# Context product of the projection blocks: one matmul of 128 weight columns, or two of 64 columns

## The reference, cut to what matters

```python
h = rms_norm(x, norm1_g) * (1 + sc1) + sh1
z = h @ w_in
conv_a, conv_g, q, k, v = jnp.split(
    z, [D_CONV, 2 * D_CONV, 2 * D_CONV + D_QK, 2 * D_CONV + 2 * D_QK], axis=-1)
```

## Time and profile before

| | |
|---|---|
| median of 3 runs | 1809.16 us (1808.12 to 1811.60) |
| profiled execution, first to last instruction (span) | 1807.7 us |
| TensorE busy | 1619.1 us, 90% |
| VectorE / ScalarE / GpSimd busy | 829.0 / 572.2 / 391.3 us |
| projection blocks (L649, L705) | 1024 passes |

### The profile page before, as it was taken

The page is one execution under the profiler, slowest core; times in us unless marked ns, Lnnn a source line. Parts: engine busy times, 40 slices in busy tenths (PEclk is TensorE's granted clock), DMA queues, the critical chain, the costliest instruction groups (busy, mean ns, idle before and its releaser), DMA issues. The chain is left out here.

```text
span 1807.7 us, 69734 instructions
## 1 busy us (share of the span) xinstructions
PE 1619.1 (90%) x27905; PEld 1281.1 (71%) x27905; DVE 829.0 (46%) x2593; ACT 572.2 (32%) x2228; POOL 391.3 (22%) x2166
## 2 busy tenths in 40 slices
PE   6999988986999999888869999899599998998885
PEld 3554457446999989888735554664389988998885
DVE  2299768262333323232245996943623232423233
ACT  2200245235545432211130003542355554221211
POOL 1100000002343424332310000000124333333332
PEclk9999999997999999999989999999799999999998
DMA  9356640237999999999953412221599999999992
GB/s 348 129 184 235 233 174 1 105 127 284 402 409 409 409 409 409 409 409 409 361 206 140 157 58 102 108 94 35 202 374 409 409 409 409 408 409 409 409 407 111
DMA packets 146722, 502.59 MB, mean 278 GB/s; under 512 B 6217, under 2 KB 6642, under 8 KB 146578
## 3 DMA queue, kind: packets, MB, share of 16 engines
q1 hardware_dynamic: 142288, 488.96, 69.5%
q0 software_dynamic: 3264, 10.88, 1.8%
q10 hardware_dynamic: 1026, 1.25, 0.2%
HBM read 494.76 MB, written 6.31 MB: 277 GB/s over the span
## 5 line engine op out<-in xcount | busy, mean ns | idle before, releaser
L950 PE MATMUL ps<-v_sb,weight_ring 128*64 128x80 f32 x16384 | 589.3, 234 | 51.7 <-DMA weight_ring<-in_w_gate_dram 20.8
L950 PEld LDWEIGHTS ps<-v_sb,weight_ring 128*64 128x64 f32 x16384 | 577.3, 138 | 63.0 <-DMA weight_ring<-in_w_gate_dram 25.0
L967 PE MATMUL ps<-v_sb,weight_ring 128*64 128x80 f32 x8192 | 296.7, 234 | 31.7 <-DVE v_sb L1693 19.9
L967 PEld LDWEIGHTS ps<-v_sb,weight_ring 128*64 128x64 f32 x8192 | 288.4, 138 | 40.0 <-DVE v_sb L1693 25.0
L705 PE MATMUL ps<-mix,weight_ring 128*128 128x128 f32 (+1 forms) x976 | 271.0, 439 | 2.1 <-ACT mix L1054 1.2
L1238 ACT ACTIVATE v_sb<-mix 128x8 f32 x1520 | 185.5, 205 | 223.6 <-PE ps L950 146.1
L1719 DVE TENSOR_TENSOR qk<-qk,v_sb 128x8 f32 x1520 | 212.3, 194 | 90.8 <-issue 90.0
L1848 POOL COPY v_sb<-mix 128x8 f32 x1040 | 145.2, 198 | 479.0 <-PE ps L950 417.7
L1861 POOL TENSOR_TENSOR qk<-qk,v_sb 128x8 f32 x1040 | 198.7, 232 | 181.7 <-DVE v_sb L1708 178.5
L705 PEld LDWEIGHTS ps<-mix,weight_ring 128*128 128x128 f32 x976 | 148.1, 194 | 122.8 <-issue 119.8
L1443 DVE SCALAR_TENSOR_TENSOR weight_ring<-u_gate,conv_cols,weight_ring 128x655 f32<-128x655 f32 x240 | 195.3, 899 | 0.0
(11 more groups left out here) (195 smaller groups left out, 1240.5 us busy)
## 6 DMA issues: line engine op xcount, KB each, us to landing
weight_ring<-in_w_down_dram SPq DMA_DIRECT2D x64, 2048.0 KB, 23.7
weight_ring<-in_w_gate_dram SPq DMA_DIRECT2D x48, 2048.0 KB, 20.9
weight_ring<-in_w_up_dram SPq DMA_DIRECT2D x48, 2048.0 KB, 23.6
weight_ring<-in_w_mod_dram SPq DMA_DIRECT2D x24, 2048.0 KB, 9.0
weight_ring<-in_w_in_dram SPq DMA_DIRECT2D x10, 2048.0 KB, 8.3
spare<-in_w_gate_dram SPq DMA_DIRECT2D x32, 512.0 KB, 10.4
weight_ring<-in_w_out_dram SPq DMA_DIRECT2D x4, 2048.0 KB, 9.4
rope_sb<-in_w_gate_dram SPq DMA_DIRECT2D x16, 512.0 KB, 11.3
```

What stands on the lines that cost most here:

```text
L950: last = nc.tensor.matmul(ps[c * HALF:(c + 1) * HALF, 2 * (i % 2) + f // BLK, f % BLK * CAP:(f % BLK + 1) * CAP], w[:, kk, o:o + HALF], pi ...
L967: last = nc.tensor.matmul(ps[c * HALF:(c + 1) * HALF, 4 + d // BLK, d % BLK * CAP:(d % BLK + 1) * CAP], w[:, kk, o:o + HALF], hid[:, k, :] ...
```

## The change

The context product of every projection block, early ones too, takes each 128-column weight piece as two pieces of 64 columns. The two matmuls stream the same 128 context tokens, and write partitions 0 to 63 and 64 to 127 of the same PSUM columns. The latent product stays a full-array matmul. Only TensorE's program changes; PSUM contents, semaphores and everything on the other engines stay.

```diff
             for l in range(DEPTH):
+                def context_product(n, w, k, b, ends):
+
+                    for c in range(2):
+                        at = b * P + c * HALF
+                        last = nc.tensor.matmul(ps[c * HALF:(c + 1) * HALF, 2 * (n % 3) + 1, 0:N_CTX], w[:, k, at:at + HALF],
+                                                mix[:, k, 0:N_CTX], start=(k == 0), stop=ends)
+                    return last
...
                             if n == 0:
                                 pe.wait_ge(*k_lo_ready.at(0, 2 * k + (1 if bank else 2)))
-                            nc.tensor.matmul(ps[:, 2 * (n % 3) + bank, 0:cols.stop - cols.start], w[:, k, tokens(b)],
-                                             mix[:, k, cols], start=(k == 0), stop=False)
+                            if bank == 1:
+                                context_product(n, w, k, b, False)
+                                continue
+                            nc.tensor.matmul(ps[:, 2 * (n % 3), :], w[:, k, tokens(b)], mix[:, k, cols],
+                                             start=(k == 0), stop=False)
...
-                            last = nc.tensor.matmul(
-                                ps[:, 2 * (n % 3) + bank, 0:cols.stop - cols.start], w[:, k, tokens(b)],
-                                mix[:, k, cols], start=(k == 0), stop=(k == KD - 1))
+                            if bank == 1:
+                                context_product(n, w, k, b, k == KD - 1)
+                                continue
+                            last = nc.tensor.matmul(ps[:, 2 * (n % 3), :], w[:, k, tokens(b)], mix[:, k, cols],
+                                                    start=(k == 0), stop=(k == KD - 1))
```

## The result

The changed kernel takes 1816.55 us (median of 5, 1812.39 to 1819.09) beside 1808.12 for the kernel before (5 runs, 1806.71 to 1811.60; the 1809.16 of the table above is the median of three of them): slower, ratio 1.0040, 95% interval 1.0028 to 1.0053. A second measurement gave 1818.10 (6 runs) beside 1807.82, ratio 1.0060 (1.0043 to 1.0077). The forecast was 1820.0 with a range of 1815.0 to 1823.5.

A forecast was written before the change was run, and what follows sets the result against it. TensorE's own pace was taken to bound the projection, carried one to one to the end. Terms 5.5 + 1.6 + 0.35 + 3.6 = 11.05 us gave a median of 1820.2, written as 1820.0 us, range 1815 to 1823.5.

The forecast's parts named there:

- Nothing but TensorE sets the end of the projection: Projection and v blocks of both layers: TensorE busy every microsecond, DMA share 0.50 or less, VectorE waiting for TensorE.
- A pair costs what a whole pass costs: Context product: two half passes side by side take 0.111 us against 0.1125 for a full-array pass, gaining 0.8 us in all.
- Entering halves 0.15, leaving 0.20 us: Array mode changes between full array and halves: pause plus exposed first weight load, 0.35 us a round trip.
- A plain block of before takes 8.67 us: Projection block without modulation rows in the kernel before: 8.67 us, read from five blocks on end taking 43.44 us.
- Plain blocks +0.325 net, 5.5 us in all: 17 blocks behind full-array work: two new mode changes each, +0.35 less the pairs' gain, +5.5 us together.
- Blocks behind modulation rows +0.12: 13 blocks behind modulation rows: strips to halves 0.15 and 0.20 out, replacing 0.20 paid before; +1.6 us together.
- Early blocks +3.6 us: Early blocks alternating modes every chunk: ten round trips on the path, 3.15 us, plus 0.45 for the half clock.
- Blocks 0 +0.35 us: Blocks 0 of both layers: entry hidden by a wait, leaving costs 0.2 each, less a smaller first load.
- One to one to the end: From projection to kernel end: every change of TensorE's projection time carries through fully, 11.05 us in all.
- tiles of 32 and 64 columns do change mode: Rival, blocks behind modulation rows: no pause between these modes, -0.02 each instead of +0.12, 1.9 us less, 1818.1; chance 0.16.
- the pauses were not hidden: Rival, mode changes: most cost hidden or absent, only loads exposed, 0.15 a round trip, ending at 1809 to 1812.8; chance 0.05.
- the granted clock stayed at full level in the blocks: Rival, projection blocks: the granted clock falls, as in the first early block, which ran at half level; chance 0.06.

The follow-up runs named there:

- the first four variants: Changed kernel again, halves in main blocks only, in early blocks only, latent product in halves too: +10.3, +5.0, +2.9, -1.7 us against the kernel before.
- halves and pairs together: Kernel before, with context and latent products in halves and modulation rows done two sets at a time: +0.1 us, ratio 0.9999.
- pairs alone: Kernel before, with only the modulation rows done two sets at a time behind every second block: -1.0 us, ratio 0.9994.

## Why the prediction was right

By its own steps:

- *Nothing but TensorE sets the end of the projection*: right. The stages grew by 9.7 us, TensorE was busy in every microsecond of the blocks again (145.07 of 145.07 us from 57.28, 158.38 of 158.38 from 941.74), and VectorE's wait for the means in layer 0 went from 6.8 to 8.8 us. In layer 1 it stayed at 3.9, where it was to grow too.
- *A pair costs what a whole pass costs*: right. Whole blocks in halves take 8.61 us where 8.65 is the time with full-array passes.
- *Entering halves 0.15, leaving 0.20 us*: right. Turning one round trip away saved 0.35, adding one cost 0.35. The parts of 0.05 and 0.105 us show in the longest passes, which leaves 0.1 us for each of the two pauses.
- *A plain block of before takes 8.67 us*: 0.02 too long. The five blocks of the earlier trace rows stand behind modulation columns, and the first of their passes lasts 357 ns where the median is 276, so 0.08 us of an exposed load is in the 43.44. It hardly moved the sum, which was added up from the price of the changes.
- *Plain blocks +0.325 net, 5.5 us in all*: +0.31 (8.96 - 8.65), and 5.0 in all. Two of the 17 stand behind modulation columns, where the kernel before paid those 0.08 us already, and cost 0.1 us less: from the columns to the next rows the five blocks of layer 1 went from 44.25 us (970.61 to 1014.86) to 45.69 (983.58 to 1029.27), 1.44 more and not 5 x 0.31. The gain of the pairs is 0.35 - 0.31 = 0.04 a block, 0.0025 us a pair of passes, where 0.0015 was forecast.
- *Blocks behind modulation rows +0.12*: 10.81 to 10.82 instead of 10.83, +0.10 to 0.11. The change between tiles of 32 and 64 columns, which no row of before showed, costs 0.15 us as assumed.
- *Early blocks +3.6 us*: the term that was most off, 2.9 us. From the first early pass to the modulation columns it was 16.48 us before (46.25 - 29.77) and is 19.40 now (51.56 - 32.16), with the same clock of 0.84 in the first 10 us. A chunk measured 1.42 us against the 1.43 forecast, so the price per trip was right. The ten trips were put at 3.15 us without the half clock and measured 2.9 with it: the 0.45 for the half clock did not show, and why not stays open, since no run separates that part. The two chunks behind the columns were hidden, as forecast: from the columns to the last wait for ScalarE it is 5.35 us in both (51.60 - 46.25, 56.91 - 51.56).
- *Blocks 0 +0.35 us*: about 0.3, by difference (9.7 - 2.9 - 5.0 - 1.4, the last for the 13 blocks behind rows).
- *One to one to the end*: within what can be told, to about a tenth. 11.05 us were forecast in the stages, 9.7 measured there, and 8.4 and 10.3 in the time.

The rivals: tiles of 32 and 64 columns do change mode; the pauses were not hidden; the halves did not share the time; and the granted clock stayed at full level in the blocks, even with twice the round trips. That the range held the first measurement by 1.5 us only comes from three things of like size: the kernel before measured 1.0 us less than the 1809.16 that the sum stood on, the stages grew by 1.4 us less than 11.05 (half of that is the early term), and the time came out 1.2 us under the stages. That all three pulled the same way, and that they stopped inside the range, is in part chance.

## What to carry to other kernels

Halving the weight columns of a matmul does not halve its time where the other half is wanted too: both halves must stream the same columns, and here the pair cost what the whole cost. (Halves that stream different columns, or that fill an array otherwise empty, were not tried.) What decides then is the number of changes of tiling mode in TensorE's order, here 0.15 to 0.20 us each in float32 with its first load: count them in the program's order, and keep products of one mode together. For effects of some microseconds, compare a stage between fixed events at full clock in two profiles; it repeated to 0.2 us here, where single run times scattered by 7.

## What the runs showed that I had not expected

- A control of the same program came out 1.0 us (0.04%, interval -0.14 to +0.05%) away from its reference, and single runs go with the mean granted clock: over the 29 reference runs of the first four variants, 0.8 us less for each thousandth more (correlation -0.76).
- With every matmul of a block in halves the block is 0.04 us faster than with full-array ones, all of it in the context part (1.75 us in halves, 1.79 in full-array passes). Why is open.
- Pauses for changes of mode did not lower the granted clock: window 57.28 to 202.35 us of the changed kernel, with two or three changes a block, has a mean clock of 1.00.
- Behind a wait of 2.3 us the clock did fall in one of two profiles (halves and pairs together, 0.83 over 10 us), and not in the other (pairs alone).
